# Issuing the stores of the state-space outputs from ScalarE's queue instead of SyncE's, in a streaming encoder layer

## What is computed

```python
z = rmsnorm(x) @ w_in                       # 1024 -> xl 512, gl 512, us 512
y_lru = rglru(conv4(xl)) * gelu(gl)         # gated linear recurrence over time
ys    = s5(us)                              # 32 groups x 16 channels, 64 complex states
g     = gelu(ys)
y_ssm = g * sigmoid(g @ w_glu + b_glu)
x = x + concat(rmsnorm(y_lru), rmsnorm(y_ssm)) @ w_out
h = rmsnorm(x)
x = x + (silu(h @ w_gate) * (h @ w_up)) @ w_down    # 22 chunks of 128
y = rmsnorm(x)
```

## Time and profile before

| | |
|---|---|
| median of 3 runs | 2249.74 us (2248.51 to 2253.14) |
| span of the profiled execution, first to last instruction | 2246.2 us |
| TensorE busy | 2195.1 us (98%) |
| VectorE, ScalarE, GpSimd busy | 1485.6 (66%), 1069.3 (48%), 363.3 us (16%) |
| hardware DMA queues used | one, SyncE's, its packets at 47.5% of the 16 transfer engines' time |

### The profile page before, as it was taken

One profiled execution on the slowest core, in us unless ns is written; L12 is line 12 of the kernel. 1 busy time (PEld: TensorE's weight loads), 2 busy tenths in 40 slices (PEclk: granted clock), 3 DMA queues, 4 the chain that ended last, 5 costly groups with the idle time before them and its releaser, 6 DMA issues.

```text
span 2246.2 us, 30290 instructions
## 1 busy us (share of the span) xinstructions
PE 2195.1 (98%) x11590; PEld 2087.1 (93%) x11590; DVE 1485.6 (66%) x2540; ACT 1069.3 (48%) x1446; POOL 363.3 (16%) x438
## 2 busy tenths in 40 slices
PE   8898999999999999999999999999999999999997
PEld 4566899999999999999999999999999999999996
DVE  6857555787566667876665687676658875665444
ACT  4427423656544456464444565444455464432232
POOL 4022100232111002411110132202102411100001
PEclk9999999999999999999999999999999999999998
DMA  7964335464335365633355556335365643343331
GB/s 237 235 213 138 118 114 135 146 189 139 122 114 181 118 148 164 185 122 118 123 172 135 148 173 175 113 113 183 113 148 148 174 121 120 113 143 114 129 117 66
DMA packets 201759, 324.52 MB, mean 144 GB/s; under 512 B 89296, under 2 KB 132944, under 8 KB 201488
## 3 DMA queue, kind: packets, MB, share of 16 engines
q1 hardware_dynamic: 201488, 322.36, 47.5%
q0 software_dynamic: 128, 0.23, 0.0%
HBM read 298.09 MB, written 26.53 MB: 145 GB/s over the span
## 4 chain that ended last, share of the span: by engine, by line
PE 88%; DVE 6%; ACT 3%; issue 1%; POOL 1%; SPq 0%; DMA 0%; POOLq 0%; DVEq 0%; ACTq 0%
PE acc L960 26%; PE acc L962 26%; PE acc L961 25%; PE acc L1052 5%; PE acc L1083 1%; PE acc L1074 1%; PE acc L1063 1%; PE acc L1073 1%; DVE rstd L1273 1%; DVE x_acc L1157 1%; DVE w_hl L1157 1%; DVE act_hl L1157 1%; POOL tmp L659 1%; ACT act_hl L935 0%; SPq L542 0%
## 5 line engine op out<-in xcount | busy, mean ns | idle before, releaser
L960 PE MATMUL acc<-act_hl,w_hl 128*128 128x416 f32 x2448 | 866.6, 354 | 6.5 <-DVE act_hl L1157 4.9
L961 PE MATMUL acc<-act_hl,w_hl 128*128 128x416 f32 x2448 | 853.3, 349 | 0.0
L962 PE MATMUL acc<-act_hl,w_hl 128*128 128x416 f32 x2448 | 853.3, 349 | 0.0
L1157 DVE TENSOR_TENSOR w_hl<-w_raw,w_hl 128x1024 fp32r<-128x1024 f32 x416 | 514.9, 1252 | 63.2 <-ACT w_hl L749 61.7
L960 PEld LDWEIGHTS acc<-act_hl,w_hl 128*128 128x128 f32 x2448 | 460.0, 188 | 15.4 <-DVE act_hl L1157 7.6
L961 PEld LDWEIGHTS acc<-act_hl,w_hl 128*128 128x128 f32 x2448 | 460.7, 188 | 2.4 <-issue 1.9
L962 PEld LDWEIGHTS acc<-act_hl,w_hl 128*128 128x128 f32 x2448 | 459.9, 188 | 1.1
L749 ACT ACTIVATE w_hl<-w_raw 128x1024 fp32r<-128x1024 f32 x416 | 431.8, 1052 | 46.0 <-DMA w_raw<-in_w_ffn 45.6
L1157 DVE TENSOR_TENSOR x_acc<-x_acc,acc 128x416 f32<-128x416 f32 x480 | 265.8, 584 | 171.6 <-PE acc L962 167.3
L960 PE MATMUL acc<-ff_hl,w_hl 128*128 128x416 f32 x880 | 312.4, 355 | 4.8 <-issue 4.3
L659 POOL TENSOR_TENSOR tmp<-tmp 128x416 f32<-128x416 f32 x117 | 147.6, 1262 | 1009.7 <-ACT tmp L760 948.8
(11 more groups left out here) (197 smaller groups left out, 1925.8 us busy)
## 6 DMA issues: line engine op xcount, KB each, us to landing
w_raw<-in_w_ffn SPq DMA_DIRECT2D x330, 512.0 KB, 3.7
w_raw<-in_w_in SPq DMA_DIRECT2D x60, 512.0 KB, 3.3
s5y<-y_dram SPq DMA_DIRECT2D x80, 256.0 KB, 4.0
w_raw<-in_w_out SPq DMA_DIRECT2D x40, 512.0 KB, 3.3
s5t<-t_dram SPq DMA_DIRECT2D x64, 162.0 KB, 3.8
s5v<-v_dram SPq DMA_DIRECT2D x80, 128.0 KB, 3.9
x_acc<-in_x SPq DMA_DIRECT2D x4, 1664.0 KB, 8.1
out_y<-x_acc SPq DMA_DIRECT2D x8, 832.0 KB, 7.1
```

Source lines behind the costliest of these rows:

```text
L960: pe.matmul(out, w(0), x(0), start=first, stop=False)
L961: pe.matmul(out, w(0), x(1), start=False, stop=False)
L962: return pe.matmul(out, w(1), x(0), start=False, stop=last)
L1157: return v.tensor_tensor(out, x, y, op)
```

## The change

Twenty `gst` steps leave SyncE's program and enter ScalarE's, at the same places of the list. Waits, transfers and semaphores are the same. `gld` stays on SyncE.

```diff
@@ sync
-                elif kind == "gst":
-                    wait_evacuated(sp, ("y5", b, 4 * j + 1))
-                    wait_evacuated(sp, ("y5", b, 4 * j + 2))
-                    wait_evacuated(sp, ("y5", b, 4 * j + 3))
-                    if b >= 2:
-                        sp.wait_ge(ys_in[j], 16 * (b - 1))
-                    for s in range(L):
-                        sp.dma_start(g_dram(b)[j, :, :, s, :].rearrange("g h c -> h g c"),
-                                     u5(b)[s * HG:(s + 1) * HG, j * GE:(j + 1) * GE, :]).then_inc(g_st[j], 16)
@@ scalar, behind the gelu of "s5"
+                elif kind == "gst":
+                    wait_evacuated(act, ("y5", b, 4 * j + 1))
+                    wait_evacuated(act, ("y5", b, 4 * j + 2))
+                    wait_evacuated(act, ("y5", b, 4 * j + 3))
+                    if b >= 2:
+                        act.wait_ge(ys_in[j], 16 * (b - 1))
+                    for s in range(L):
+                        act.dma_start(g_dram(b)[j, :, :, s, :].rearrange("g h c -> h g c"),
+                                     u5(b)[s * HG:(s + 1) * HG, j * GE:(j + 1) * GE, :]).then_inc(g_st[j], 16)
```

## The result

| | median us | runs | from to |
|---|---|---|---|
| before | 2249.62 | 11 | 2248.03 to 2253.14 |
| after | 2253.87 | 11 | 2251.83 to 2257.09 |

The ratio is 1.0022, with an interval of 1.0014 to 1.0031; the medians are 4.25 us apart. The forecast was 2257.5, in a range of 2252.0 to 2262.5. "Slower" meant over 0.2%, and the ratio stands just on that side of it (the quotient of the medians alone is 1.0019); its interval has both. The median lies nearer to the first rival's 2252 to 2253 than to the forecast's 2257.5.

The account below looks back on a forecast made before the run. TensorE, busy 98% of the span, was taken to bound the kernel. Terms of 0 and 6.8 (block 0), 1.0 (block 1) and 0 (blocks 2 to 4) gave +7.8 us: 2257.5 us, range 2252.0 to 2262.5.

Parts of the forecast that it names:

- first rival: ScalarE's queue issues beside unfinished arithmetic, so block 0's `gst` 2 costs nothing: +2.3 to +3.3 us, 2252 to 2253; 17%.
- The place: End of block 0's mixer, 190 to 210 us: ScalarE has no slack and two moved steps fall there; +6.8 us.
- The price of a step: Each moved step's eight issues hold ScalarE for 3.7 us, from nothing to 5.05 us at the bounds.
- `glu`'s term: Block 0's last two steps make the last quarter, and so `glu`, late: +6.8 us.
- block 1's term: Block 1's first step delays an evacuation by 2.0 us and a recurrence by 1.0 us: +1.0 us on the kernel.
- What SyncE gains I cost at nothing: SyncE loses 74 us of issues and sends loads up to 3.7 us sooner, but TensorE waits for no load: 0.
- slow-issue rival: Issues are slower from ScalarE, since both queues share what makes transfers or wait for room: +11.8 us, 2261.5 us; 13%.
- Blocks 2 to 4: Twelve steps hidden in ScalarE's idle time before its next PSUM evacuation: cost nothing.
- the first two steps of block 0: Over by 169.9 us, ahead of ScalarE's evacuation at 171.99, so hidden in its idle time: 0.
- SyncE's freedom: Rival in which earlier loads give back 4.5 us of TensorE's time: faster, 2244 us; 2%.
- its own range: 2255.5 to 2260 us, allowing a 1 us gap in ScalarE's chain and a longer lower clock before `glu`.

Follow-up runs that it names:

- e1_block0: Kernel before with ScalarE issuing only block 0's four `gst` steps, SyncE the sixteen others: 2254.88 us, +5.16 over before.
- e2_rest: Kernel before with ScalarE issuing only the sixteen `gst` steps of blocks 1 to 4, block 0's staying on SyncE: 2249.99 us, +0.27 over before.
- g1_after: The changed kernel run once more, unaltered, in another set of rounds: 2254.44 us, +4.75 over before.
- e5_drained: Changed kernel, with block 0's `gst` 2 and `gst` 3 each waiting for the ScalarE instruction just ahead to finish: 2256.30 us, +6.81 over before.
- e6_early: Changed kernel with block 0's `gst` 2 issued earlier on ScalarE's queue, right behind the step `wc` 2: 2252.40 us, +2.91 over before.
- e8_double: Changed kernel with each transfer of block 0's `gst` 2 and `gst` 3 cut in two, 16 issues a step: 2259.43 us, +9.94 over before.

## Why the prediction was right, and where it was off

**The place: right.** The loss is in the last two steps of block 0 (e1_block0, e2_rest). "A microsecond put on ScalarE there is a microsecond on the kernel" holds here within some 0.5 us: the last part of `glu` is late by 4.27 us, and 4.25 us were timed. That these two are so near is luck; the same kernel in g1_after has 5.2 and 4.75.

**The price of a step: the mis-sized term.** The step that failed is "in every list of work so far one instruction follows another, and I see no reason for an exception", by which a step holds ScalarE for all of its 3.7 us of issuing. It held it for 2.25 us (`gst` 2) and 2.93 us (`gst` 3), since the queue starts issuing beside the instructions ahead. e5_drained takes that away and comes to the forecast's picture: 3.91 and 5.11 us of standstill (the second with a stretched issue), `glu` 7.2 us late, 2256.3 us. Along the chain the difference adds up: 3.8 became 2.35 us at the copy, and `gst` 3, starting during the squares instead of behind them, ended 5.1 us late instead of 8.0. That is the 2.5 us by which `glu`'s term was too large (6.8 against 4.3), and it is most of the 3.6 us; block 1's term is about the rest.

**A term put at nothing: the loads that SyncE sends sooner.** "What SyncE gains I cost at nothing", and the slow-issue rival was discounted because SyncE "has little to issue from 196 to 207 us". The one weight load that lay there went out among the stores of `gst` 3, and the last of these landed 4.6 us behind its issue instead of 1.7. The forecast had the high part late by as much as the last issue. That came out nearly so (5.45 and 5.1 us), but by luck: 2.55 us more for the landing, 2.2 us less for the load behind it.

**Block 1: 1.0 us forecast, none found.** The evacuation was 1.1 us late and not 2.0, and TensorE's wait of 1.27 us took it. Blocks 2 to 4 cost nothing that e2_rest can tell, as said, and the first two steps of block 0 nothing on ScalarE's chain: the copies around them, at 145.40, 162.27 and 170.47, stand 16.87 and 8.20 us apart, and 16.86 and 8.21 before (146.92, 163.78, 171.99).

**The first rival was half right.** That the issues run beside arithmetic is what the trace shows, and its bound for deciding was near: ScalarE held "for less than some 2.5 us a step", the loss under 4.5 us. It was held for 2.25 and 2.93 us, and the loss is 4.25, so the forecast has the direction by a narrow margin and the rival the nearer number. But its sum, 2.3 to 3.3 us, let `gst` 2 cost nothing and `gst` 3 wait only for GpSimd's sum. The run-ahead covers two or three issues of eight; the other five or six stand ahead of everything behind them. The Trainium skill (Advanced Engine Details and Errata, "Sequencer and Instruction Queues") has the sequencer push an engine instruction into a queue, where it waits for its semaphores and resources, and read the next. The rows of after agree, with issues from 189.18 on beside a table load and two square roots that end at 190.73.

**Slower issues: not as a rule, but now and then.** The median is 0.455 us. Yet `gst` 3 took 3.83 us in the profile of the changed kernel and 5.67 us in that of the same kernel in g1_after, where the timeline has

```profile
200.03 4.66 ACTq L905 DMA_DIRECT2D g_first<-u_first  x6
204.74 0.96 ACT L847 ACTIVATE zs_next<-acc 128x416 f32<-128x416 f32 x1 [4.78 <-issue]
```

One issue of 2.24 us delays the copy of `us` by as much as it is stretched. The same place has one issue of 1.69 to 2.07 us in e5_drained, e6_early and e8_double. In all four the stretched issue overlaps the flight of SyncE's weight load, but in six other profiles with that load in flight none is stretched; the cause was not tried.

**SyncE's freedom gave nothing that shows:** e2_rest has sixteen steps off SyncE and ends at 2249.99. The Trainium skill (DMA: Bandwidth & Descriptors, "Issuing engines are not separate DMA queues") says that issue time is usually small beside the transfer. For one transfer this case agrees (0.455 us of issuing, 2.9 us to landing), and to that extent the prediction set the wrong two numbers beside each other. For the eight of a step it doesn't: they are issued one after another in 3.7 us while their flights overlap, and doubling the issues at the same bytes cost 5.6 us (e8_double).

**The clock:** the prediction had a longer time at its lower level as a part of its own range. The trace has it (half clock to 217 us and not to 210), the times don't show that it counts.

**What stays open:** whether the two steps cost more together (4.25 to 5.2 us) than the sum of each alone (3.0 us); the noise doesn't settle it. Candidates are the order (`gst` 2 moves `gst` 3 later), the stretched issues, and the weight load among the stores, which has no run of its own. And the share of the clock, above.

## What to carry to other kernels

A DMA issue is work on the engine whose queue makes it: count issues, not bytes, and look at what stands behind them in that engine's order, not at its share of busy time. ScalarE is idle for half of this kernel, and sixteen of twenty steps were free; four stood in block 0, and two of these, where ScalarE has no gap, were the loss as far as the traces show. Ask also what the queue that was relieved sends out sooner, and whether the moved transfers now share the way with it. Before pricing a step at its full issue time, look at what stands ahead of it: what is still at work when the queue gets there covers the first few issues, and where the instruction behind waits for something else anyway, nearly all of them (e6_early).

## What the hardware showed

- ScalarE's queue began issuing 1.55 us before the end of the arithmetic ahead of it (189.18 against 190.73), past three instructions that hadn't finished; in none of the stretches shown did an instruction behind the issues start before the last of them had ended.
- An issue on ScalarE's queue took 0.455 us in the median, against 0.431 on SyncE's, and its data landed 2.9 us after it, against 2.3. At the last step of block 0 the difference goes with what else is in flight: stores issued ahead of SyncE's weight load landed in 1.6 to 1.9 us from either queue, the three that ScalarE issued behind it in 3.1 to 4.6 us.
- Single issues on ScalarE's queue stretched to 1.98 us in the changed kernel and to 2.24 us in g1_after. The eight of the first step of block 0 took 5.33 us and held ScalarE for 5.20, at no cost there; one of SyncE's own issues took 1.76 us in the same stretch (at 148.28).
- The changed kernel's times follow the mean granted clock of TensorE: 2255.94 to 2257.09 us in its three runs at 0.990, 2251.83 and 2252.83 in its two at 0.993. Which is the cause of which no run here shows.
